# Two reorderings in a two-block transformer kernel: a step's row sums behind its side work, and a gain row behind the rests of the weights

## Chip, cores and metric
The kernel runs on one core of a Trainium2 chip. The metric is the device time of one execution in microseconds (us), the median of several runs. Engines are called by the profile's names: PE is TensorE (matrix products; PEld is its weight load), DVE is VectorE, ACT is ScalarE, POOL is GpSimd, and SP is the engine that issues most of the transfers.

## What is computed
Two blocks of two layers each run one after the other on 256 tokens (two tiles of 128, `NT = 2`) with a model width of 1024. The first block has a latent stream `x` and a context stream `ctx`; the second has one stream, with a mixture of experts at its end. What matters here:

```python
mod_l = silu(c) @ w_mod[l] + b_mod[l]            # first block: six rows of 1024 per layer
mod   = c_act @ w_ada[layer] + b_ada[layer]      # second block: a_shift, a_scale, a_gate, f_shift, ...
x_lat = x_lat + g1_l * rmsnorm(m_l, norm_mix_post[l])
f_l   = rmsnorm(x_lat, norm_ffn_pre[l]) * (1.0 + sc2_l) + sh2_l
x_lat = x_lat + g2_l * rmsnorm(swiglu(f_l, w_gate[l], w_up[l], w_down[l]), norm_ffn_post[l])
h     = h + f_gate * swiglu_2(u, ffn_w_gate[0], ffn_w_up[0], ffn_w_down[0])
```

`swiglu(h, wg, wu, wd)` is `(silu(h @ wg) * (h @ wu)) @ wd` with an inner width of 2816.

## The kernel before
**Exact products from three.** A float32 operand is split into an upper part, rounded by ACT (`high_*`), and a lower rest, which DVE subtracts (`low_*`). `products3` (lines 553 to 555) then adds three products: upper by upper, upper by rest, rest by upper. So each tile of weights costs a transfer (SP), an upper part (ACT, 1.9 us) and a rest (DVE, 2.3 us) before PE can use it.

**A dense line** (`class Line`) is one swiglu. It runs in steps of 256 inner columns, 11 steps per stream: the first line has two streams (22 steps), the second and third have one each (11 steps). The first lies at about 370 to 780 us, the second at 1036 to 1230, the third at 1375 to 1560. In step `n` PE does `up(n, 0)` and `up(n, 1)` (gate and up products of the two token tiles, 24 products each), small transposes `turn` of the hidden values through PSUM bank 6, and `downs(n - 1)` (24 products). DVE and ACT work on the next weights and the last hidden values. `fetch_w(n + 2)` (four transfers, 2 MB) and `fetch_d(n + 1)` (one, 1 MB) are issued by SP, each behind the semaphore that frees its buffer: the first behind `up(n, 1)`, the second behind `downs(n - 1)`. Each engine works through its instructions strictly in the order in which the program writes them, SP too.

**Side work.** `beside(n)` advances a generator by one piece, three times per step. In the first line it holds the norms, residual sums and transposes of the tokens of the other stream (`beside_first`): steps 0 to 5 and, after a pause, steps 12 to 17. In the second and third lines it is over after step 0.

**Row sums.** The modulation rows of the second block are row sums of `w_dots` times the condition, done by DVE in the lines. One `dot` multiplies a 128x1024 tile by the condition and adds up each row (112 in all; `tensor_tensor_reduce`, the rows `CUSTOM_DVE_ANT_0` of the profile), and then issues the next tile's transfer (512 KB) on SP into the buffer just read. There are two such buffers. `condition(n, long)` does two dots: with `long=False` ("early" below) after `split_h(n - 1, 1)`, only if no side work is under way, and with `long=True` ("late") after `split_h(n, 0)`, always. At n = 0 it only issues the first two transfers. A step without side work has four dots. The first line does 48, the second and third 32 each, up to their last step but two.

**The second output product** (`joint_out`, l = 1, at 1000 to 1050 us) multiplies the mixer's result by `w_out` in two halves of columns and two token tiles (`piece(j, t4)`). `row_gain` multiplies the gate row (broadcast from memory by POOL) by the norm row (transferred by SP) into a gain row, which `from_banks` uses in the token's residual sum. `split(1, h)` gives the two halves of the second half of `w_out`. `line.fetch_w(0)`, `high_w` and `low_w` prepare the first weights of the line that follows. `keep_busy` are products without use, which fill waits of PE.

Of the kernel before, what the change touches and what calls it, by code (L numbers as in the profile page):

```python
# [119 lines left out]
def build(nc, i, out):  # L120
# [150 lines left out]
    def bank_for_pe(b):  # L271
        pe.wait(*bank_free[b])
        return psum[:, b, :]
# [4 lines left out]
    def keep_busy(b, n):  # L278

        bk = bank_for_pe(b)  # L280
        for _ in range(n):
            t.matmul(bk[:, 0:256], ident[:], bc(ident[:], 1, 2), start=True, stop=True)
# [267 lines left out]
    def products3(out_, hi, lo, w_hi, w_lo, start, stop):  # L550

        hi, lo, w_hi, w_lo = (one_pass(z) for z in (hi, lo, w_hi, w_lo))
        t.matmul(out_, hi, w_hi, start=start, stop=False)  # L553
        t.matmul(out_, hi, w_lo, start=False, stop=False)  # L554
        return t.matmul(out_, lo, w_hi, start=False, stop=stop)  # L555
# [146 lines left out]
    def shape_condition():  # L702

        if broad[1]:
            broad[2] = ac.put(a.activation, cond, cond, ACT.Silu, after=[broad[1]])
            broad[1] = None

    def fetch_dot(limit):

        n = dot_asked[0]  # L710
        if n < limit:
            dot_asked[0] += 1
            slot = dot_slots[n % 2]
            sp.wait(slot.reader)
            nc.sync.dma_start(slot.ap[:], dot_rows[n // KD, :, n % KD, :]).then_inc(slot.sem, 16)
            slot.n += 16
            dot_there[n] = (slot.sem, slot.n)
# [126 lines left out]
    def finish_off(chain):  # L844
        for _ in chain:
            pass

    def to(chain, name):

        for r in chain:  # L850
            if r == name:
                return
        assert False, name

    def preload(function):

        loaded[0] += 1
        ac.put(a.activation, tables[:, loaded[0]:loaded[0] + 1], ident[:, 0:1], function)

    class Line:  # L860
# [128 lines left out]
        def run(self, streams, side, fetch_next, split_next, last_chain, waiting=None, root_first=False):  # L989

            self.streams, self.summed = streams, {}
            self.up_, self.down_, self.gate_, self.hidden_, self.turn_, self.h_split = {}, {}, {}, {}, {}, {}
            self.hi_free = pe.now()
            not_yet, beside_busy = [0], [bool(side)]

            def beside(n):
                if side and n >= not_yet[0]:  # L1000
                    r = next(side, "over")
                    not_yet[0] = r if isinstance(r, int) else 0
                    beside_busy[0] = r != "over" and not not_yet[0]

            def condition(n, long):

                if n == 0:
                    for slot in dot_slots:
                        slot.reader = self.up_[0, 1]
                        fetch_dot(self.dots)  # L1010
                elif n < end - 1 and (long or not beside_busy[0]):
                    for _ in range(2):
                        dot(self.dots)

            self.fetch_w(1)
            self.fetch_d(0)
            self.fetch_d(1)
            end = self.n - 1
            for n in range(self.n):
                self.up(n, 0)  # L1020
                if n == 0 and waiting:
                    finish_off(waiting)
                if n:
                    self.high_d(n - 1)
                    self.low_d(n - 1)
                if n == end:
                    self.high_d(n)
                self.high_w(n + 1, 0)
                self.gate(n, 0)
                if n:  # L1030
                    self.turn(n - 1, 1)
                if n == end:
                    self.low_d(n)
                self.low_w(n + 1, 0)
                self.hidden(n, 0)
                if n:
                    self.split_h(n - 1, 1)
                if n == end:
                    break
                if n == end - 1:  # L1040
                    self.downs(n - 1, (0, 1))
                    self.fetch_d(n + 1)
                if n:
                    condition(n, False)
                beside(n)
                self.up(n, 1)
                self.high_w(n + 1, 1)
                shape_condition()
                self.gate(n, 1)
                self.low_w(n + 1, 1)  # L1050
                self.hidden(n, 1)
                self.fetch_w(n + 2)
                self.turn(n, 0)
                self.split_h(n, 0)
                condition(n, True)
                beside(n)
                if n and n < end - 1:
                    self.downs(n - 1, (0, 1))
                    self.fetch_d(n + 1)
                if n == end - 1:  # L1060
                    fetch_next(0)
                beside(n)


            if side:
                finish_off(side)
            self.downs(end - 1, (0,), range(3))
            self.turn(end, 0)
            self.split_h(end, 0)
            self.downs(end - 1, (0,), range(3, 4))  # L1070
            self.downs(end, (0,))
            if split_next:
                split_next()
            p_ = end // self.per
            preload(ACT.Sqrt)
            chains = [last_chain(0, self.summed[p_, 0])]
            to(chains[0], "rooted" if root_first else "added")
            self.up(end, 1)
            fetch_next(1)
            preload(ACT.Silu)  # L1080
            self.gate(end, 1)
            if root_first:
                to(chains[0], "turn")
            self.hidden(end, 1)
            if not root_first:
                to(chains[0], "rooted")
            self.downs(end - 1, (1,), range(3))
            self.turn(end, 1)
            self.split_h(end, 1)
            self.downs(end - 1, (1,), range(3, 4))  # L1090
            to(chains[0], "late" if root_first else "turn")
            self.downs(end, (1,))
            fetch_next(2)
            return chains[0], last_chain(1, self.summed[p_, 1])
# [631 lines left out]
    def joint_out(l, cat4, keep, fetched, line, ready):  # L1726
# [33 lines left out]
        def split(j, half):  # L1760
            low_part(j, half, high_part(j, half))
# [13 lines left out]
        def piece(j, t4, between=None):  # L1775
            b = 2 * t4 + j - (4 if l == 1 else 0)
            bk, q = bank_for_pe(b), slice(t4 * P, (t4 + 1) * P)
            if (l, j, t4) == (1, 1, 2):
                keep_busy(b, 14)
            pe.wait(cat_split[t4])  # L1780
            for k in range(KD):
                if k == KD // 2 and between:
                    between()
                pe.wait(w_low[j, k // 4])
                mm = products3(bk, xhi[:, k, q], xlo[:, k, q], his[j][:, k, :], parts[j][k // 4][:, k % 4, :], k == 0, k == KD - 1)
            mm.then_inc(pe.sem, 1)
            pe.n += 1
            done[j, t4] = pe.now()

        def row_gain(u, n):  # L1790

            (_, s, blk), g_u = asked[u]
            g = grow[:, g_u, :]
            return g, [ve.put(v.tensor_tensor, g, g, prow[:, n, :], ALU.mult, after=[(s_row, rows[0]), (s_grow[g_u], grow_n[g_u])])]

        def own_banks(tt):
            return psum[:, 2 * tt:2 * tt + 2, :].rearrange("p b n -> p (b n)")
# [6 lines left out]
        def from_banks(s, tt, gain, sets, ready_, t0=0, early=(), busy=0):  # L1804

            t4 = 2 + tt if l else tt
            marks = (done[0, t4], done[1, t4])
            squared = list(early) + row_squares(tt, range(len(early), 2))
            return onward(s, tt, own_banks(tt), marks, squared, gain, spare[:, tt, :], sets,
                          (2 * tt, 2 * tt + 1), ready_, (2 * tt, 2 * tt + 1), t0, busy)  # L1810
# [21 lines left out]
        if l == 0:  # L1832
            gain = row_gain(0, 0)
# [37 lines left out]
            return squared, row_gain  # L1871
        keep.reader = pe.now()
        line.fetch_w(0)
        gain = row_gain(0, 0)
        split(1, 0)
        split(1, 1)
        sets = [[(1, xhi[:, :, tt * P:(tt + 1) * P], xlo[:, :, tt * P:(tt + 1) * P])] for tt in range(NT)]
# [3 lines left out]
        preload(ACT.Sqrt)  # L1881
        line.low_w(0, 0)
        piece(1, 2)
        c0 = from_banks(LAT, 0, gain, sets[0], ready[LAT])
        to(c0, "turn")
        line.low_w(0, 1)
# [793 lines left out]
    lat_squares, row_gain = joint_out(0, cat4, keep, fetched, line, there)  # L2680
# [63 lines left out]
    waiting, row_gain = joint_out(1, cat4, keep, fetched, line, there)  # L2744
# [618 lines left out]
    def moe(c):  # L3363
# [201 lines left out]
        with nc.Fori(0, NEXP) as e:  # L3565
            run(e)
# [75 lines left out]
```

## Time and profile before
| | us |
|---|---|
| median of 3 runs (lowest, highest) | 2771.52 (2766.29, 2773.17) |
| the profiled execution, its own time | 2772.69 |
| its span in the trace | 2771.4 |
| PE busy | 2620.0 (95%) |
| DVE busy | 2125.7 (77%) |
| ACT busy | 1486.9 (54%) |
| mean granted clock of PE | 0.969 |

A busy share is over the whole span. Much of it is the expert stage from 1770 us on, which the change doesn't touch. Of the chain that ended last, PE has 76%, DVE 13%, ACT 7%, DMA 2%. A row of a timeline gives start, duration, engine, line, operation, output and inputs, and in brackets how long the engine had been idle before it and what ended that. Lines 76, 553 to 555, 559 and 563 are helpers that issue most of the instructions, so rows are told apart by their tiles: `wslot` are gate and up weights, `dslot` down weights, `ld_hi` the down weights' upper part, `whi` the upper part of the others, `lhb` hidden values, `lhl` the lower rest of the transposed hidden values (the last operation of `split_h`), `dot` the tiles of the row sums.

### The profile page before, as it was taken

Reading aid. Unit: us, or ns where it says so; the run is one execution under the profiler, and the core shown is the slowest. Engines: PE = TensorE matmul, PEld = TensorE weight load, DVE = VectorE, ACT = ScalarE, POOL = GpSimd, SP = SyncE. Lnnn points to the kernel's source line nnn. Section 1 sums busy time; section 2 is a strip of 40 time slices with the busy share of each in tenths; the row PEclk is TensorE's granted clock in tenths of the full one; section 3 lists DMA queues with packets and bytes.
Section 4 is the critical chain, followed back from the end, with each engine's and each line's share of the span. In section 5 each row is a group of like instructions: output and inputs, shape, how many; then the busy total and the mean of one; then the engine's idle time right before and its main releaser. Section 6 shows DMA issues by size and latency. Waiting matters only on the chain.

```text
span 2771.4 us, 32200 instructions
## 1 busy us (share of the span) xinstructions
PE 2620.0 (95%) x12954; PEld 2132.0 (77%) x12954; DVE 2125.7 (77%) x2511; ACT 1486.9 (54%) x1665; POOL 110.6 (4%) x145
## 2 busy tenths in 40 slices
PE   7989998998998889999999999999999999999997
PEld 4767676887777678877788777788888888888886
DVE  4555566787647657868688667799999999999997
ACT  4332364445443244344633526677667776767674
POOL 4023100000000300000000000000000000000000
PEclk9999899999999989999999999999999999999999
DMA  7543545885553036952289340599999999999994
GB/s 277 183 156 122 190 166 191 299 304 203 180 210 122 1 121 240 327 197 95 96 305 328 136 175 31 185 371 364 351 367 368 353 362 365 362 354 367 369 364 189
DMA packets 290442, 675.24 MB, mean 244 GB/s; under 512 B 16726, under 2 KB 113158, under 8 KB 271344
## 3 DMA queue, kind: packets, MB, share of 16 engines
q1 hardware_dynamic: 285152, 664.35, 65.9%
q0 software_dynamic: 4272, 7.72, 1.1%
q8 instruction: 104, 1.70, 0.2%
q10 hardware_dynamic: 864, 1.06, 0.1%
q14 instruction: 50, 0.41, 0.0%
HBM read 671.98 MB, written 1.10 MB: 243 GB/s over the span
## 4 chain that ended last, share of the span: by engine, by line
PE 76%; DVE 13%; ACT 7%; DMA 2%; issue 1%; SPq 0%; POOL 0%; ACTq 0%; DVEq 0%; POOLq 0%
PE psum L553 21%; PE psum L555 21%; PE psum L554 21%; PE psum L76 7%; DVE wslot_r L563 3%; PE psum L1524 1%; PE psum L396 1%; ACT whi_r L76 1%; PE psum L1663 1%; DVE cacc L76 1%; PE psum L3063 1%; DVE dslot_r L563 1%; DMA first<-in_w_mod 1%; PE psum L2091 1%; DVE x L76 1%
## 5 line engine op out<-in xcount | busy, mean ns | idle before, releaser
L553 PE MATMUL psum<-whi_r,xhi_r 128*128 128x512 f32 (+1 forms) x752 | 295.5, 393 | 12.0 <-DVE wslot_r L563 5.4
L563 DVE TENSOR_TENSOR wslot_r<-wslot,whi_r 128x2048 fp32r<-128x2048 f32 (+1 forms) x114 | 255.6, 2252 | 61.5 <-ACT whi_r L76 61.1
L555 PE MATMUL psum<-whi_r,xlo_r 128*128 128x512 f32 (+1 forms) x752 | 290.4, 386 | 0.0
L554 PE MATMUL psum<-wslot_r,xhi_r 128*128 128x512 f32 (+1 forms) x736 | 283.7, 385 | 0.0
L76 ACT ACTIVATE whi_r<-wslot 128x2048 fp32r<-128x2048 f32 (+1 forms) x114 | 212.6, 1878 | 50.8 <-DMA wslot<-in_w_up 19.5
L563 DVE TENSOR_TENSOR wslot_r<-wslot,arena_r 128x2048 fp32r<-128x2048 f32 x85 | 194.0, 2288 | 18.7 <-ACT arena_r L3022 18.1
L563 DVE TENSOR_TENSOR ring_r<-ring,wide_r 128x2048 fp32r<-128x2048 f32 x84 | 191.8, 2288 | 17.8 <-ACT wide_r L3022 16.6
L563 DVE TENSOR_TENSOR wslot_r<-wslot,wide_r 128x2048 fp32r<-128x2048 f32 x83 | 189.7, 2288 | 16.7 <-ACT wide_r L3022 16.3
L563 DVE TENSOR_TENSOR ring_r<-ring,arena_r 128x2048 fp32r<-128x2048 f32 x84 | 191.6, 2287 | 11.6 <-ACT arena_r L3022 10.8
L3022 ACT ACTIVATE arena_r<-wslot 128x2048 fp32r<-128x2048 f32 x85 | 162.3, 1917 | 68.6 <-PE psum L555 45.6
L3022 ACT ACTIVATE arena_r<-ring 128x2048 fp32r<-128x2048 f32 x84 | 160.5, 1918 | 69.3 <-PE psum L555 48.5
L3022 ACT ACTIVATE wide_r<-ring 128x2048 fp32r<-128x2048 f32 x84 | 160.7, 1918 | 67.9 <-PE psum L555 45.5
L3022 ACT ACTIVATE wide_r<-wslot 128x2048 fp32r<-128x2048 f32 x83 | 158.7, 1918 | 71.3 <-PE psum L555 49.9
L553 PEld LDWEIGHTS psum<-whi_r,xhi_r 128*128 128x128 f32 x752 | 144.8, 193 | 47.7 <-DVE dslot_r L563 4.4
L555 PEld LDWEIGHTS psum<-whi_r,xlo_r 128*128 128x128 f32 x752 | 143.9, 191 | 27.8
L554 PEld LDWEIGHTS psum<-wslot_r,xhi_r 128*128 128x128 f32 x736 | 141.3, 192 | 25.6
L76 ACT ACTIVATE ld_hi_r<-dslot 128x2048 fp32r<-128x2048 f32 x44 | 83.8, 1912 | 139.5 <-PE psum L555 139.5
L563 DVE TENSOR_TENSOR dslot_r<-dslot,ld_hi_r 128x2048 fp32r<-128x2048 f32 x44 | 100.6, 2291 | 74.3 <-ACT ld_hi_r L76 74.3
L76 DVE CUSTOM_DVE_ANT_0 dot<-dot,stage 128x1024 f32<-128x1024 f32 x112 | 134.1, 1220 | 19.1 <-DMA dot<-in_w_dots 18.9
L553 PE MATMUL psum<-ld_hi_r,lhT_r 128*128 128x512 f32 x352 | 144.1, 409 | 1.4 <-DVE lhl_r L563 1.4
L555 PE MATMUL psum<-ld_hi_r,lhl_r 128*128 128x512 f32 x352 | 140.4, 399 | 0.0
L554 PE MATMUL psum<-dslot_r,lhT_r 128*128 128x512 f32 x352 | 140.1, 398 | 0.0
(540 smaller groups left out, 6334.5 us busy)
## 6 DMA issues: line engine op xcount, KB each, us to landing
wslot<-in_moe_w_gate SPq DMA_DIRECT2D x29, 2048.0 KB, 8.0
ring<-in_moe_w_down SPq DMA_DIRECT2D x29, 2048.0 KB, 8.3
dot<-in_w_dots SPq DMA_DIRECT2D x112, 512.0 KB, 6.1
wslot<-in_moe_w_up SPq DMA_DIRECT2D x28, 2048.0 KB, 8.5
ring<-in_moe_w_up SPq DMA_DIRECT2D x28, 2048.0 KB, 8.8
ring<-in_moe_w_gate SPq DMA_DIRECT2D x27, 2048.0 KB, 8.2
wslot<-in_moe_w_down SPq DMA_DIRECT2D x27, 2048.0 KB, 8.1
dslot<-in_w_mod SPq DMA_DIRECT2D x42, 1024.0 KB, 4.8
```

The costliest lines, as they stand in the source:

```text
L76: f(*a, **k).then_inc(self.sem, 1)
L396: mm = t.matmul(psum[32 * g:32 * g + 32, MB, :], cs[:, k, :], slot.ap[:, g * 512:(g + 1) * 512], start=fresh, stop=ends, tile_position=(0, ...
L553: t.matmul(out_, hi, w_hi, start=start, stop=False)
L554: t.matmul(out_, hi, w_lo, start=False, stop=False)
L555: return t.matmul(out_, lo, w_hi, start=False, stop=stop)
L563: return v.tensor_tensor(one_pass(lo), src, one_pass(hi), ALU.subtract)
L1524: mm = t.matmul(psum[:, 3, h * HD:(h + 1) * HD], PTj[:, buf, c0:c0 + P], kvd[:, kb, 128 + g * HD:128 + (g + 1) * HD], start=(kb == 0), sto ...
L1663: mm = t.matmul(o[:, h * HD:(h + 1) * HD], dec[:, d, h, :], xdt[:, d, h * HD:(h + 1) * HD], start=(d == 0), stop=(d == 1))
L2091: mm = t.matmul(psum[:, 6, (h % 8) * HD:(h % 8 + 1) * HD], PkT[:, buf, c0:c0 + P], vals(br, kb, h // 4), start=(kb == 0), stop=(kb == nb - 1))
L3022: a.activation(one_pass(hi_of(c, g, half)), raw(c, g, half), ACT.Copy).then_inc(a_high, 1)
L3063: mm = t.transpose(psum[:, 4, k * P:(k + 1) * P], hb4[:, k:512:4], ident[:])
```

## The change
In `Line.run` the late row sums keep their place at n = 0 (where they only issue transfers) and move for all other steps behind the last `beside(n)`, that is behind the step's side work and behind `downs(n - 1)` and `fetch_d(n + 1)`. In `joint_out` for l = 1 the product that makes the gain row moves from in front of `split(1, 0)` to behind `line.low_w(0, 0)` and `piece(1, 2)`. No operation is added or taken away.

```diff
                 self.turn(n, 0)
                 self.split_h(n, 0)
-                condition(n, True)
+                if n == 0:
+                    condition(n, True)
                 beside(n)
                 if n and n < end - 1:
                     self.downs(n - 1, (0, 1))
                     self.fetch_d(n + 1)
                 if n == end - 1:
                     fetch_next(0)
                 beside(n)
+                if n:
+                    condition(n, True)
...
         keep.reader = pe.now()
         line.fetch_w(0)
-        gain = row_gain(0, 0)
         split(1, 0)
         split(1, 1)
...
         line.low_w(0, 0)
         piece(1, 2)
+        gain = row_gain(0, 0)
         c0 = from_banks(LAT, 0, gain, sets[0], ready[LAT])
```

## Rows read from the trace of the kernel before

**Rows 1.** Busy time by stretch: PE, PEld, DVE, ACT, POOL; clock, DMA share, GB/s.
```profile
370.00:580.00 210.00, 194.46 (x848) 158.98 (x848) 153.35 (x215) 98.30 (x107) 1.08 (x2) 0.97 0.71 248
1050.00:1130.00 80.00, 80.00 (x362) 66.25 (x362) 64.82 (x80) 33.48 (x29) 0.00 (x0) 1.00 0.82 286
```

**Rows 2.** Chain of waits, 380 to 720 us: start, duration, what.
```profile
407.91 1.13 DVE dot L76
...
453.78 1.14 DVE dot L76
...
627.78 1.14 DVE dot L76
...
692.50 1.14 DVE dot L76
```

**Rows 3.** PE's timeline in the first line: rows with idle time before them.
```profile
423.29 0.71 PE L76 MATMUL psum<-c_ident,ysb 128*128 128x128 f32 x4 [2.11 <-DVE lhl_r L563]
...
465.22 0.70 PE L76 MATMUL psum<-c_ident,lhb 128*128 128x128 f32 x2 [4.89 <-DVE lhl_r L563]
...
482.67 1.12 PE L76 MATMUL psum<-c_ident,ysb 128*128 128x128 f32 x4 [3.86 <-DVE lhl_r L563]
...
644.20 0.51 PE L76 MATMUL psum<-c_ident,lhb 128*128 128x128 f32 x2 [2.02 <-DVE lhl_r L563]
...
669.06 0.71 PE L76 MATMUL psum<-c_ident,ysb 128*128 128x128 f32 x4 [1.50 <-DVE lhl_r L563]
...
706.75 0.71 PE L76 MATMUL psum<-c_ident,ysb 128*128 128x128 f32 x4 [2.82 <-DVE lhl_r L563]
```

**Rows 4.** Busy time by stretch behind two of these gaps; the clock is third last.
```profile
424.10:427.50 3.40, 3.40 (x10) 2.62 (x9) 2.71 (x8) 0.63 (x1) 0.00 (x0) 0.50 1.08 379
...
644.20:648.20 4.00, 4.00 (x18) 3.35 (x19) 0.73 (x4) 3.13 (x4) 0.00 (x0) 1.00 1.08 371
```

**Rows 5.** SP's timeline in the second line: transfers issued.
```profile
1089.02 3.25 SPq L715 DMA_DIRECT2D dot<-in_w_dots  x2
1092.31 0.43 SPq L898 DMA_DIRECT2D dslot<-in_w_down  x1
...
1174.13 0.43 SPq L898 DMA_DIRECT2D dslot<-in_w_down  x1
```

**Rows 6.** DMA issues at 1089.02, 1092.31 and 1174.13: KB, us to landing.
```profile
dot<-in_w_dots SPq DMA_DIRECT2D x1, 512.0 KB, 9.0
...
dslot<-in_w_down SPq DMA_DIRECT2D x1, 1024.0 KB, 9.3
...
dslot<-in_w_down SPq DMA_DIRECT2D x1, 1024.0 KB, 9.0
```

**Rows 7.** ACT's timeline in the second line.
```profile
1089.16 1.92 ACT L76 ACTIVATE ld_hi_r<-dslot 128x2048 fp32r<-128x2048 f32 x1 [5.39 <-PE psum L555]
1094.02 1.92 ACT L76 ACTIVATE whi_r<-wslot 128x2048 fp32r<-128x2048 f32 x1 [2.95 <-DMA wslot<-in_w_up]
...
1106.05 1.92 ACT L76 ACTIVATE ld_hi_r<-dslot 128x2048 fp32r<-128x2048 f32 x1 [5.39 <-PE psum L555]
```

**Rows 8.** DVE's timeline, first line and second line.
```profile
414.30 2.29 DVE L563 TENSOR_TENSOR dslot_r<-dslot,ld_hi_r 128x2048 fp32r<-128x2048 f32 x1 [3.22 <-ACT ld_hi_r L76]
...
1083.27 1.22 DVE L76 CUSTOM_DVE_ANT_0 dot<-dot,stage 128x1024 f32<-128x1024 f32 x1
...
1099.30 1.22 DVE L76 CUSTOM_DVE_ANT_0 dot<-dot,stage 128x1024 f32<-128x1024 f32 x1
...
1165.72 1.22 DVE L76 CUSTOM_DVE_ANT_0 dot<-dot,stage 128x1024 f32<-128x1024 f32 x1
```

**Rows 9.** Timelines of DVE, PE and ACT in the second output product.
```profile
1012.84 1.23 DVE L76 TENSOR_TENSOR grow<-grow,prow 128x1024 f32<-128x1024 f32 x1 [7.34 <-DMA prow<-in_norm_ffn_post]
...
1016.32 0.50 PE L553 MATMUL psum<-whi_r,xhi_r 128*128 128x512 f32 x1 [2.34 <-DVE dslot_r L563]
...
1018.24 1.92 ACT L76 ACTIVATE first_hi_r<-wslot 128x2048 fp32r<-128x2048 f32 x1 [0.81 <-DMA wslot<-in_w_up]
```

## Prediction
> **What bounds the kernel now.** I read the chain of waits first, then busy time by stretch, then the timelines of PE, DVE, ACT and SP inside the dense lines, and last the transfers. TensorE sets the end nearly everywhere: in the second dense line it is busy without a gap, 80.00 of 80 us, while DVE is busy for 64.82 [rows 1]. The third line repeats this. In the first line (370 to 790 us) it is not so: TensorE does 194.46 of 210 us in its first half, and the chain of waits leaves it for DVE and ACT, the moved row sums among them (at 407.91, 453.78, 627.78 and 692.50) [rows 1, 2]. The gaps are on TensorE's own timeline, each ended by `lhl_r`, the lower rest that frees bank 6 for the next transpose: 2.11, 4.89, 3.86, 2.02, 1.50 and 2.82 us [rows 3]. Behind that of 2.11 us the granted clock is at its lower level, 1.2 GHz (0.50), for 3.4 us; behind that of 2.02 us it stays at 1.00 [rows 4]. A product lasts twice as long at the lower level, so each such stretch costs 1.7 us more.
>
> **Part 1, row sums behind the side work, on DVE.** No instruction is added or removed: the row sums remain, at 1.22 us each [rows 8]. Per step n >= 1 two of them (2.3 us, with a closing sum of 0.5 us now and then) move from behind `split_h(n, 0)` to behind the step's last `beside`. Where no side work is left, DVE's order doesn't change at all. Where there is, the side's small DVE operations run 2.3 us sooner, so do ACT's scaling and `high_d` behind them, and the row sums fall into the time in which DVE waits for `ld_hi`. DVE shows this hole: the sums at 407.91 are on the chain [rows 2], end at 410.2, and then DVE waits 3.22 us for ACT's `ld_hi` until 414.30 [rows 8]. Step by step:
> - Step 1: DVE's chain comes 2.3 us sooner, but the next transposes also wait for `up(2, 1)` through gate, hidden and split (some 1.5 us, as the gap of 1.50 us shows [rows 3]): 2.11 us becomes 1.5, gain 0.6.
> - Step 3: the sums at 453.78 lead to the gap of 4.89 us. The whole 2.3 us are gained.
> - Step 4: DVE waits there for TensorE's transposes, not for the sums. The 3.86 us stay, gain 0.
> - Step 13: the sums at 627.78 and their closing operations are 2.8 us in front of the tile's norm. 2.0 us are gained at 644.20, and the other 0.8 at the gap after it, some 15 us later, which DVE's weights' rests end.
> - Step 15: the sums move into the wait for `ld_hi`. Gain 0.
> - Step 16: the sums up to 692.50 lead to the gap of 2.82 us, whose floor is again some 1.1 to 1.5. Gain 1.7.
> - Step 17: now the sums stand behind the gain row at the step's end and hold back `low_d`, where TensorE's reserve was 1.3 us. Loss 0.9.
> Sum: 0.6 + 2.3 + 2.8 + 1.7 - 0.9 = 6.5 us gained. Of the low stretches behind the gaps of 2.11 and 2.82 us one or both should go, since gaps of 1.50 and 2.02 us had none: 1.7 to 3.4 us at best; I take 1.7. **First line: 8.2 us faster**, between 3 (the floors are higher) and 11.
>
> **Part 1, the same move on SP.** `dot` also issues the next row's transfer, and SP works in order. Before, both transfers of a step were issued as soon as the sums were done, and `fetch_d(n + 1)` (1 MB of down weights) behind them: at 1089.02 the two rows, at 1092.31 the weights [rows 5]. Now `fetch_d` stands first. It waits for `downs(n - 1)`, which end when ACT's `ld_hi` starts, 1089.16 [rows 7], and the second sum was done only at 1091.9, so the weights go out about 3 us sooner and the rows behind them. The transfers are at that time queued up: the first row landed 9.0 us after its issue (1098.0), the weights 9.3 after theirs (1101.6) [rows 6]. With the second row, 1.2 us behind the first (an estimate: half a MB), the landings follow the order of issue: 1098.0, 1099.2, 1101.6. So 1 MB is worth 2.4 us, and with the weights first the rows land at 1100.4 and 1101.6.
> Who waits: the next step's two sums, at 1099.30 and 1.14 behind it [rows 8]. They had 1.3 and 1.2 us of reserve, and now wait for about 1.2. Behind them on DVE are `low_w(n + 1, 1)`, `hidden(n, 1)`, `split_h(n, 0)`; behind them on SP is `fetch_w(n + 2)`, which already lands just in time (ACT waits 2.95 us for it at 1094.02 [rows 7]). One such delay is hidden by reserve. The question is whether it adds up. A round of transfers, from the end of a step's early sums (the second starts at 1083.27, at 1165.72) to the landing of its weights, took 1084.4 to 1101.6 in the first and 1166.9 to 1183.1 in the last of six steps [rows 5, 6, 8]: 17.2 and 16.2, mean 16.6 us. Before, the sums didn't wait for the end of it. Now the last thing to land is the row that the second sum needs, so a round is closed: 16.6 + 1.2 (that sum) = 17.8 us, against TensorE's 16.9 per step (1089.16 to 1106.05 [rows 7]). TensorE's transposes of the second tile half came at about 1100.1 (5.9 before 1106.05) and needed the split that ended at 1099.3: reserve 0.8 us, which the first two waits use up. Then each step with four sums costs 0.9 us: seven such steps (n = 2 to 8), 6.2 us in the second line and the same in the third: **12.4 us slower**, from 0 (rounds shorter than 15.7 us) to 20 (17.2 each).
> In the first line steps 6 to 12 also have four sums, but `fetch_w` goes there at TensorE's pace and the reserve in front of the split is 3 us: I count 0 (at most 2). On POOL four of the late sums' steps store a finished gate row; POOL does nothing else of weight there, and the row is read only in the next stage: 0.
> The Trainium skill ("DMA: Bandwidth & Descriptors", Queues, rings and completion order) says that each DMA engine consumes descriptors in ring order, but that completion is not first-in first-out per issuing engine. By the first half the rows wait for all of the weights, as in the sum; by the second a row could overtake. The order of landings just given agrees with the first.
>
> **Part 2, the gain row.** `gain` waits 7.34 us for the norm rows, until 1012.84, and takes 1.23; the two rests of `w_out`, which need nothing of it, stand behind it, and TensorE's piece waits 2.34 us for them until 1016.32. Moved behind `low_w(0, 0)` and `piece(1, 2)`, the rests come 8 us sooner and the piece 2.3. But the chain that leads on from there starts at ACT, which waits for the line's first weights until 1018.24 [rows 9], takes 1.92 us for their upper part and then a table load of 1.3, so it squares from 1021.6 on, both halves by 1022.7; the piece ended at about 1022.0 (24 products of 0.23 us from 1016.32), so ACT was no earlier anyway. The gain row lies in the time in which DVE waits for those squares. What TensorE wins it stands idle some 10 us later, in front of the first tile's transposes, which wait for ACT and DVE. I count 0: at best 0.3, at worst 1.7, if that new gap brings the lower clock. SP's order doesn't change (the gain issues nothing).
>
> **Sum.** -8.2 + 12.4 + 0 = +4.2 us on the profiled execution's 2772.69 us (span 2771.4 and 1.3 around it): 2776.9, I say **2777**. That execution lies in the spread of the runs (median 2771.52, 2766.29 to 2773.17). About 0.3%, 8.3 us, is what a measurement can tell from no change.
>
> **Rivals.**
> - *Only the gain.* Landings don't bind: TensorE's pace keeps the rounds at 16.9 because a later start finds an emptier queue. For it: the six rounds vary by 1 us, and at 15.7 the drift is nil. Against it: the early sums had only 1.2 us of reserve and the weights take 2.4. Then -8.2: 2764.5. 22%.
> - *Slower by more than can be missed.* The closed round decides in lines two and three from the step on in which the split comes behind TensorE's transposes. At the 17.2 us of the first round it loses 1.5 us per step, 14 steps, 20 us less the 8.2: 2785; gaps of 2 us would bring lower clock on top. For it: the first round itself, and no reserve left in the early sums. 22%.
> - *Nothing moves.* The side work gets its 2.3 us but other gaps give them back (ACT's tables, the clock's phase), and DMA reserve suffices: 2772. 8%.
> - *The forecast case*, -2 to +10 us around +4.2: 48%, own range 2770 to 2782.
>
> **How the numbers follow.** Faster by over 0.3%: half of the first rival and a little of the forecast case, 0.13. Slower: the second rival and a sixth of the forecast case, 0.30. The rest, 0.57, within. For 8 in 10: 2763 to 2787.
>
> **What would show it.** In the changed trace: SP issues `dslot` before the two rows in each step; the row sums behind `split_h(n - 1, 1)` in the second line wait for DMA (before: none there), 1 us and more; ACT's `ld_hi` rows in that line come every 17.5 to 17.8 us instead of 16.9; TensorE has gaps of about 0.9 us there. In the first line the gaps at 465, 644 and 706 us shrink by 2.3, 2.0 and 1.7, that at 482 stays. TensorE's piece after the fill starts at about 1014, and the next stage no sooner than before. I am wrong if `ld_hi` keeps 16.9 us in line two, or if the first line doesn't get shorter by 5 us or more.

## The result and the profile after

| | before | changed |
|---|---|---|
| median, lowest and highest (us) | 2770.81 (2766.29, 2773.17) | 2788.36 (2782.30, 2791.43) |
| ratio, with its 95% interval | | 1.0048 (1.0030, 1.0066) |
| span in the trace | 2771.4 | 2790.1 |
| mean granted clock | 0.969 | 0.969 |

The medians are those of six runs of each kernel. The change makes the kernel slower, by 13.3 us by the ratio (8.3 to 18.3) and 17.5 by the medians. Forecast was 4.2 us slower: the side is right, the size is a third of the measured one by the ratio and a quarter by the medians. The changed median lies above the prediction's range of 2763 to 2787 us; by the ratio on the 2771.5 us of before it would be 2784.8, inside that range and outside the forecast case's own 2770 to 2782.

The chain that ended last is where one looks first. The part of the page after that gives its shares; before, DMA had 2% of it and the rows' transfers had no entry of their own.

```profile
PE 66%; DVE 14%; DMA 9%; ACT 6%; SPq 3%; issue 1%; POOL 0%; ACTq 0%; DVEq 0%; POOLq 0%
PE psum L553 18%; PE psum L555 17%; PE psum L554 17%; PE psum L76 7%; DMA dot<-in_w_dots 6%; DVE wslot_r L563 3%; DVE dot L76 2%; SPq L887 1%; PE psum L1527 1%; SPq L898 1%; PE psum L396 1%; DMA wslot<-in_w_up 1%; ACT whi_r L76 1%; PE psum L2094 1%; DVE cacc L76 1%
```

Busy time by stretch in the same stretches as [rows 1], and the clock behind two gaps that answer to those of [rows 4]: in the first line TensorE is busy for 2.8 us more of 210, the second has lost its full 80 us, and no low clock is left behind the gap at 417.74.

```profile
370.00:580.00 210.00, 197.25 (x865) 161.00 (x864) 153.42 (x210) 99.88 (x102) 1.07 (x2) 0.98 0.72 249
...
1050.00:1130.00 80.00, 78.43 (x351) 64.08 (x350) 61.02 (x77) 30.14 (x24) 0.00 (x0) 1.00 0.82 295
...
417.70:421.70 4.00, 3.96 (x19) 3.37 (x20) 2.06 (x5) 0.63 (x1) 0.00 (x0) 1.00 1.02 352
```

TensorE's timeline in the first line after, rows with idle time before them, to be laid beside [rows 3]. 2.11 has become 1.49, 4.89 has become 2.62, 3.86 stays, 2.82 has become 1.49, and 0.94 is new at step 17, all as forecast. But 2.02 has not gone (2.48), and 0.91 at 583.88 is new.

```profile
417.74 0.71 PE L76 MATMUL psum<-c_ident,ysb 128*128 128x128 f32 x4 [1.49 <-DVE lhl_r L563]
...
455.77 0.51 PE L76 MATMUL psum<-c_ident,lhb 128*128 128x128 f32 x2 [2.62 <-DVE lhl_r L563]
...
473.43 0.91 PE L76 MATMUL psum<-c_ident,ysb 128*128 128x128 f32 x4 [3.86 <-DVE lhl_r L563]
...
583.88 0.51 PE L76 MATMUL psum<-c_ident,lhb 128*128 128x128 f32 x2 [0.91 <-DVE lhl_r L563]
...
638.27 0.50 PE L76 MATMUL psum<-c_ident,lhb 128*128 128x128 f32 x2 [2.48 <-DVE lhl_r L563]
...
699.11 0.71 PE L76 MATMUL psum<-c_ident,ysb 128*128 128x128 f32 x4 [1.49 <-DVE lhl_r L563]
...
717.91 0.51 PE L76 MATMUL psum<-c_ident,lhb 128*128 128x128 f32 x2 [0.94 <-DVE lhl_r L563]
```

The second line after, first SP: `fetch_d` (L898) at 1099.92, the two rows behind it at 1102.42; in [rows 5] it was the other way round. The transfers issued there took, to their landing, 10.1 us and 8.9 us (median of two).

```profile
1099.92 2.46 SPq L898 DMA_DIRECT2D dslot<-in_w_down  x1
1102.42 1.34 SPq L715 DMA_DIRECT2D dot<-in_w_dots  x2
```
```profile
dslot<-in_w_down SPq DMA_DIRECT2D x1, 1024.0 KB, 10.1
...
dot<-in_w_dots SPq DMA_DIRECT2D x2, 512.0 KB, 8.9
```

DVE in the same round: the early sum at 1111.27 had to wait 1.05 us for its row, a wait that the same sum at 1099.30 in [rows 8] did not have. It comes in every step of the line from n = 2 to n = 8.

```profile
1109.80 0.42 DVE L563 TENSOR_TENSOR lhl_r<-psum,lhT_r 128x256 fp32r<-128x256 f32 x1
1111.27 1.22 DVE L76 CUSTOM_DVE_ANT_0 dot<-dot,stage 128x1024 f32<-128x1024 f32 x1 [1.05 <-DMA dot<-in_w_dots]
...
1112.51 1.23 DVE L76 CUSTOM_DVE_ANT_0 dot<-dot,stage 128x1024 f32<-128x1024 f32 x1
```

The transfers don't fill the round in either kernel. From 1112 to 1113 us, while the next rows and weights can't yet be issued, the DMA share is 0.01; before, it was 0.10 at the same place of the round (1100 to 1101 us). So the round is long because its parts wait for one another, not because the DMA engines are always full.

ACT behind it: `ld_hi` came every 16.9 us [rows 7] and now has 17.57 and 17.93 us between these three, and `whi` waits 4.13 and 4.48 us for weights that `fetch_w` asked for late.

```profile
1080.88 1.92 ACT L76 ACTIVATE ld_hi_r<-dslot 128x2048 fp32r<-128x2048 f32 x1 [5.39 <-PE psum L555]
1086.92 1.92 ACT L76 ACTIVATE whi_r<-wslot 128x2048 fp32r<-128x2048 f32 x1 [4.13 <-DMA wslot<-in_w_up]
...
1098.45 1.92 ACT L76 ACTIVATE ld_hi_r<-dslot 128x2048 fp32r<-128x2048 f32 x1 [6.08 <-PE psum L555]
1104.85 1.92 ACT L76 ACTIVATE whi_r<-wslot 128x2048 fp32r<-128x2048 f32 x1 [4.48 <-DMA wslot<-in_w_up]
...
1116.38 1.92 ACT L76 ACTIVATE ld_hi_r<-dslot 128x2048 fp32r<-128x2048 f32 x1 [6.44 <-PE psum L555]
```

TensorE's timeline in the second output product after: the wait of 2.34 us in front of the piece [rows 9] is gone, and in its place stands one of 2.04 us in front of the next transposes, which wait for ACT.

```profile
1021.62 1.30 PE L76 MATMUL psum<-c_ident,ysb 128*128 128x128 f32 x8 [2.04 <-ACT ysb L76]
```

**A yardstick for each line.** The first `ld_hi` of a line and the one of its last-but-one step (the 21st of the first line, the tenth of the second and third) mark the line's length. In the trace of before, in order of the lines: 371.1, 152.0 and 152.1 us.

```profile
394.59 1.90 ACT L76 ACTIVATE ld_hi_r<-dslot 128x2048 fp32r<-128x2048 f32 x1
765.72 1.91 ACT L76 ACTIVATE ld_hi_r<-dslot 128x2048 fp32r<-128x2048 f32 x1
...
1055.35 1.91 ACT L76 ACTIVATE ld_hi_r<-dslot 128x2048 fp32r<-128x2048 f32 x1
1207.36 1.91 ACT L76 ACTIVATE ld_hi_r<-dslot 128x2048 fp32r<-128x2048 f32 x1
1384.99 1.91 ACT L76 ACTIVATE ld_hi_r<-dslot 128x2048 fp32r<-128x2048 f32 x1
1537.04 1.91 ACT L76 ACTIVATE ld_hi_r<-dslot 128x2048 fp32r<-128x2048 f32 x1
```

After: 368.1, 160.9 and 161.6 us.

```profile
389.62 1.90 ACT L76 ACTIVATE ld_hi_r<-dslot 128x2048 fp32r<-128x2048 f32 x1
757.74 1.91 ACT L76 ACTIVATE ld_hi_r<-dslot 128x2048 fp32r<-128x2048 f32 x1
1047.04 1.91 ACT L76 ACTIVATE ld_hi_r<-dslot 128x2048 fp32r<-128x2048 f32 x1
1207.97 1.91 ACT L76 ACTIVATE ld_hi_r<-dslot 128x2048 fp32r<-128x2048 f32 x1
1390.13 1.91 ACT L76 ACTIVATE ld_hi_r<-dslot 128x2048 fp32r<-128x2048 f32 x1
1551.69 1.91 ACT L76 ACTIVATE ld_hi_r<-dslot 128x2048 fp32r<-128x2048 f32 x1
```

So the lines account for -3.0 + 8.9 + 9.5 = +15.4 us. The two profiled executions differ by 18.7. The other 3.3 us are a sum of larger parts: -5.0 in front of the first line, -0.3 between the first and the second (the gain row's place), +4.5 between the second and the third, and +4.1 behind the third. The change touches none of these but the second. e2 below shows parts of the same size: the kernel with the gain row alone was profiled at a span of 2778.0 us, 6.6 above before, and its median is that of before.

### The profile page after: what moved, and what is told of

It is laid out like the page before. It is cut to its first block, busy times and chain, and to the rows that moved or that the text cites. A ratio compares the mean times of both kernels' runs of the same rounds, so it can differ in the third digit from the quotient of the medians.

```text
span 2790.1 us, 32200 instructions
## 1 busy us (share of the span) xinstructions
PE 2627.2 (94%) x12954; PEld 2134.3 (76%) x12954; DVE 2129.2 (76%) x2511; ACT 1488.4 (53%) x1665; POOL 110.3 (4%) x145
## 4 chain that ended last, share of the span: by engine, by line
PE 66%; DVE 14%; DMA 9%; ACT 6%; SPq 3%; issue 1%; POOL 0%; ACTq 0%; DVEq 0%; POOLq 0%
PE psum L553 18%; PE psum L555 17%; PE psum L554 17%; PE psum L76 7%; DMA dot<-in_w_dots 6%; DVE wslot_r L563 3%; DVE dot L76 2%; SPq L887 1%; PE psum L1527 1%; SPq L898 1%; PE psum L396 1%; DMA wslot<-in_w_up 1%; ACT whi_r L76 1%; PE psum L2094 1%; DVE cacc L76 1%
## 5 line engine op out<-in xcount | busy, mean ns | idle before, releaser
L563 DVE TENSOR_TENSOR wslot_r<-wslot,arena_r 128x2048 fp32r<-128x2048 f32 x85 | 194.1, 2288 | 16.1 <-ACT arena_r L3025 15.1
L563 DVE TENSOR_TENSOR ring_r<-ring,wide_r 128x2048 fp32r<-128x2048 f32 x84 | 191.8, 2288 | 16.4 <-ACT wide_r L3025 15.2
L563 DVE TENSOR_TENSOR wslot_r<-wslot,wide_r 128x2048 fp32r<-128x2048 f32 x83 | 189.6, 2288 | 18.8 <-ACT wide_r L3025 17.8
L3025 ACT ACTIVATE wide_r<-ring 128x2048 fp32r<-128x2048 f32 x84 | 160.5, 1918 | 69.5 <-PE psum L555 51.2
L555 PE MATMUL psum<-arena_r,xf_lo_r 128*128 128x512 f32 x340 | 132.8, 391 | 0.0
```

The source lines that it names most:

```text
L563: return v.tensor_tensor(one_pass(lo), src, one_pass(hi), ALU.subtract)
L3025: a.activation(one_pass(hi_of(c, g, half)), raw(c, g, half), ACT.Copy).then_inc(a_high, 1)
```

## The experiments

Line lengths are by the yardstick above, in us. Each experiment's ratio is against the kernel before on the same chip.

| kernel | median | ratio (95%) | line 1 | line 2 | line 3 |
|---|---|---|---|---|---|
| before (trace) | 2771 to 2773 | | 371.1 | 152.0 | 152.1 |
| changed | 2788.36 | 1.0048 (1.0030, 1.0066) | 368.1 | 160.9 | 161.6 |
| e1: DVE new, SP old | 2765.04 | 0.9974 (0.9958, 0.9990) | 362.3 | 152.0 | 152.6 |
| e2: gain row alone | 2769.68 | 0.9999 (0.9984, 1.0014) | 371.2 | 152.0 | 152.0 |
| e4: DVE old, SP new | 2793.25 | 1.0078 (1.0061, 1.0095) | 374.2 | 160.5 | 162.0 |
| e5: first line only | 2770.69 | 0.9997 (0.9985, 1.0009) | 368.0 | 152.0 | 152.0 |
| e6: half rows | 2763.47 | 0.9960 (0.9945, 0.9975) | 364.6 | 152.0 | 152.0 |
| e7: steps 1 to 5 | 2781.05 | 1.0028 (1.0014, 1.0042) | 365.7 | 159.5 | 156.9 |
| e8: e1, old from step 17 | 2767.17 | 0.9975 (0.9961, 0.9989) | 361.0 | 152.2 | 152.0 |
| e9: rows on POOL | 2772.13 | 1.0000 (0.9983, 1.0016) | 364.4 | 155.6 | 155.2 |
| e10: steps 6 to 8 | 2769.06 | 0.9981 (0.9966, 0.9997) | 368.2 | 156.5 | 155.0 |
| e11: steps 1 to 7 | 2786.43 | 1.0050 (1.0030, 1.0071) | 365.9 | 159.2 | 164.3 |
| e12: e1 without gain row | 2762.41 | 0.9960 (0.9942, 0.9977) | 362.3 | 152.0 | 152.0 |

The theory: DVE's new order is a gain in the first line, SP's new order is a loss in all three, and the loss comes from bytes in the queue. The rival: DVE's order, or the clock, makes the loss. The forecast counted parts one by one ("term" below is one part of that sum); the experiments take them apart.

**DVE's order without SP's (e1).** In the changed kernel:

```diff
                 if n and n < end - 1:
                     self.downs(n - 1, (0, 1))
-                    self.fetch_d(n + 1)
...
                 if n:
                     condition(n, True)
+                if n and n < end - 1:
+                    self.fetch_d(n + 1)
```

> The changed kernel with fetch_d(n + 1) issued behind the late row sums, so that SP's order is again that of before (two rows, then 1 MB of down weights) while DVE's order is the changed one. Theory (the loss is SP's order: the rows stand behind the weights in the queue and the next step's early sums wait for them): ACT's ld_hi rows in the second and third line come every 16.9 us again, TensorE's gaps of 0.4 to 2.0 us there are gone, the two lines give back 8.9 and 9.6 us. The first line keeps the 3 us that it won. Total about 3 us below the kernel before (2766 to 2771), 15 to 20 below the changed one. Rival (the loss is DVE's order, or the phase of the clock, and the queue only shows it): the lines stay at 161 us from first to last ld_hi instead of 152, total 2782 to 2790.

Measured: 2765.04 us, 7.2 faster than before (2.8 to 11.6) and 20 to 23 faster than the changed kernel. The second and third line are back at 152. The rival falls. The total is just below the expected 2766 to 2771. The first line is 8.8 us shorter than before, not 3: the expectation took it from the changed kernel, and so missed that SP's order costs 5.8 us there too. In the first line of e1 the gap at step 13 is gone (2.0 us), and the one after it, 3.66 us at 659.54 before, is smaller by 0.4 of the 0.8 that was forecast. TensorE's timeline of e1, the whole of its gaps from 560 to 656 us:

```profile
648.09 0.69 PE L76 MATMUL psum<-c_ident,ysb 128*128 128x128 f32 x2 [3.26 <-DVE lhl_r L563]
```

**SP's order without DVE's (e4).** In the kernel before, the late sums stay, and their two transfers are issued at the end of the step, behind `fetch_d`.

```diff
-                        dot(self.dots)
+                        dot(self.dots, not long)
...
                 beside(n)
+                if n and n < end - 1:
+                    for _ in range(2):
+                        fetch_dot(self.dots)
```

> The kernel before with SP's order alone: the late sums stay where they were on DVE, the transfers of the next two rows are issued at the step's end, behind fetch_d. Theory: ld_hi every 17.5 us and more in the second and third line, about 9 us lost in each, nothing won in the first: 18 us slower than before, 2786 to 2793, at or above the changed kernel. Rival (DVE's order decides): ld_hi stays at 16.9 and the total within 3 us of before.

Measured: 2793.25 us, 21.6 slower (16.9 to 26.3): 8.5 and 10.0 us in the second and third line as expected, and 3.1 in the first, where the expectation had no loss. With e1 this closes the square. In the second and third line SP's order by itself makes the whole loss (8.5 and 10.0 against 8.9 and 9.5). In the first line the two orders don't simply add up: -8.8 (e1) and +3.1 (e4) make -5.7, and the changed kernel has -3.0. SP's order costs 3.1 us there behind DVE's old order and 5.8 behind the new one; in steps 6 to 11 e4 loses 0.2 us and the changed kernel 1.9.

**The gain row alone (e2).** Only the second hunk of the diff.

> The kernel before with part 2 alone (the gain row behind the weights' rests). Theory of the prediction: TensorE's piece starts 2.3 us sooner and the first tile's transposes no sooner, 0 us in total (0.3 better to 1.7 worse). Rival (the 4.5 us that the changed kernel lost between the second and third line, and 4.0 behind the third, at lower granted clock, belong to this part): the total is 3 us or more slower.

Measured: ratio 0.9999 (0.9984, 1.0014), so nothing within 4 us. Its profiled execution lost 5.5 us between the second and third line and 3.9 behind the third (by the yardstick), as the changed kernel's did, at a lower clock (0.70 from 1300 to 1345 us, before 0.81), and its median still doesn't move: those differences are one execution's and not the gain row's.

**First line only (e5).** `first` is true where a line has two streams.

```diff
-                if n == 0:
+                if n == 0 or not first:
                     condition(n, True)
...
-                if n:
+                if n and first:
                     condition(n, True)
```

> The changed kernel with the late sums at the step's end in the first line only, at the old place in the second and third; part 2 is in it. Theory: the second and third line as before (152 us from first to last ld_hi), the first line 3 us shorter as in the changed kernel: 2766 to 2770. Against the first kernel of this set it keeps the new order on SP in the first line, which the theory prices at 2 us (steps 6 to 12 of the changed kernel lost 1.9 us). Rival: the 4 to 5 us that the changed kernel lost outside the lines stay here too, and the total is 2774 or more.

Measured: 2770.69 us, no difference from before (-4.2 to +2.5), the second and third line at 152.0, the first at 368.0 as in the changed kernel. Against e1, which differs only in SP's order in the first line (in the other two no side work is left, so both run both engines' old order), that is 5.7 us by the lines and 5.7 by the medians. The price of SP's order in the first line is shown, and the 2 us of theory are wrong (the rival's 2774 or more is wrong too). ACT's timeline says where it is paid. The first fence is e1 at step 12, where the side work sets in again; the second is the changed kernel at the same step.

```profile
605.46 1.92 ACT L76 ACTIVATE ld_hi_r<-dslot 128x2048 fp32r<-128x2048 f32 x1 [2.97 <-PE psum L555]
607.28 1.90 ACT L76 ACTIVATE whi_r<-wslot 128x2048 fp32r<-128x2048 f32 x1
...
625.14 1.90 ACT L76 ACTIVATE ld_hi_r<-dslot 128x2048 fp32r<-128x2048 f32 x1
```
```profile
607.20 1.92 ACT L76 ACTIVATE ld_hi_r<-dslot 128x2048 fp32r<-128x2048 f32 x1 [2.48 <-PE psum L555]
613.19 1.92 ACT L76 ACTIVATE whi_r<-wslot 128x2048 fp32r<-128x2048 f32 x1 [4.07 <-DMA wslot<-in_w_up]
...
630.67 1.90 ACT L76 ACTIVATE ld_hi_r<-dslot 128x2048 fp32r<-128x2048 f32 x1
```

In e1 `whi` follows `ld_hi` at once; in the changed kernel it waits 4.07 us for weights, and the norms of the side work, which stand behind it on ACT and DVE, are late: 23.5 us from `ld_hi` to `ld_hi` against 19.7. The rounds of steps 6 to 11 had built up that delay (`whi` comes 2.5, 3.2, 5.3, 5.8, 6.6 and 5.7 us behind `ld_hi`, in e1 always 1.8 but for 2.2 at the first) while TensorE lost only 1.9 us of it (in e1 nothing).

**Half the bytes (e6).** In the changed kernel a row's transfer brings 512 of 1024 columns, and the sum is made twice over them; the modulation rows are then not those of the reference.

```diff
-            nc.sync.dma_start(slot.ap[:], dot_rows[n // KD, :, n % KD, :])...
+            nc.sync.dma_start(slot.ap[:, 0:512], dot_rows[n // KD, :, n % KD, 0:512])...
```

> The changed kernel with half of each row's bytes: a row transfer brings 256 KB instead of 512, and its sum is made in two operations over the same half, so that DVE's time stays about the same (the modulation rows are then not those of the reference). Theory (a closed round of transfers: 5 MB per step, 17.6 us from the end of a step's early sums over rows, weights and rows to the next): four half rows take 4 x 0.6 = 2.4 us out of the round, 15.2 us is below TensorE's 16.9, ld_hi comes every 16.9 us in all three lines. The second and third line last 152 us, the first 362 as with SP's old order (in the changed kernel 368), and the total is that of the first kernel of the first set, 2760 to 2768. Rival (the loss is the wait for the semaphore and the order of SP's instructions, not bytes): ld_hi stays at 17.6 us and the total at 2780 or more.

Measured: 2763.47 us, 11.1 faster than before (6.9 to 15.2), all rounds of the second and third line at 16.9, and step 12 of the first at 19.7 as in e1. SP's order is the changed one, and it costs nothing here. So it is the length of the round, not the order as such: a smaller row shortens it, whether by its bytes alone or by what a shorter transfer also saves the transfers behind it. The first line is 364.6 instead of 362: a gap of 4.15 instead of 3.85 us at step 4 and one step at 28.9 instead of 27.2 are left unexplained.

**The rows on their own queue (e9).** `fetch_dot` in the changed kernel:

```diff
-            sp.wait(slot.reader)
-            nc.sync.dma_start(slot.ap[:], ...
+            po.wait(slot.reader)
+            nc.gpsimd.dma_start(slot.ap[:], ...
```

> The changed kernel with the rows' transfers issued by POOL on its own queue instead of SP; the weights stay on SP. Theory: the rows no longer stand behind the weights' 1 MB, and SP's fetch_w no longer waits for the early sums, so the round is open: ld_hi every 16.9 us, 152 us in the second and third line, the first as with SP's old order, total 2760 to 2768. Rival (one set of DMA engines serves both queues at about the rate at which it is now filled, so a row queued second still comes second or the rows slow the weights): 17.3 us and more per step, 2780 and more.

Measured: 2772.13 us, as before (-4.7 to +4.4). The middle of the expectation holds: from the second `ld_hi` to the ninth the period is 16.9 us again. The edit does two things at once, and the run doesn't separate them: the rows leave the queue of the 1 MB, and SP issues `fetch_w` without waiting for the sums. That a row gets past the weights shows at one place, by little: weights issued at 1114.76 land at 1124.1, a row issued by POOL at 1115.16 lands at 1123.5. Its edges don't: the first period is 18.8 us in the second line and 19.1 in the third, the last 18.4 and 17.8. At the start POOL issues two rows while SP's queue still holds the first weights, and ACT's `whi` at 1052.66 waits 5.46 us for its own (in the changed kernel 3.23 at that place). The first line is 2.1 us longer than e1's. The total is therefore above the 2768 that was expected.

**A part of the steps (e7, e10, e11).** All three are the changed kernel with the late sums at the step's end only in the steps named, in the second and third line.

```diff
-                if n == 0:
+                behind = n and (len(streams) == 2 or n < 6)    # e7; e10: n > 5; e11: n < 8
+                if not behind:
                     condition(n, True)
```

> The changed kernel, but in the second and third line the late sums stand at the step's end in steps 1 to 5 only and at the old place from step 6 on (the first line is unchanged from the changed kernel). Theory: three rounds of 17.6 us in each line lose 0.7 each, 2 to 2.5 us per line; with SP's old order from step 6 the queue catches up, ld_hi comes every 16.9 us again, and the loss of the last two steps (1.3 and 3.6 us in the changed kernel's second line), which is the lag meeting the step in which the down products come before up(n, 1), is gone. Each line 154.5 us from first to last ld_hi, total 4 to 5 us above the version with the first line only, 2773 to 2777. Rival (the end of the line costs 4 to 5 us by itself, whatever came before, or the lag stays): 157 us and more per line, 2780.

Measured: 2781.05 us, missed by 4. The lines are 159.5 and 156.9, both longer than the expected 154.5; lines and total are what the rival said (157 and more, 2780). Five periods are long (17.8 18.0 18.2 17.8 18.0 in the second line), not three, since a round's delay arrives two steps after it; then come 16.9 and, in the last, 19.0. SP's old order stops the loss but doesn't give the queue its reserve back. That made me form the theory of the next two.

> The changed kernel, but in the second and third line the late sums stand at the step's end in steps 6 to 8 only (the other half of the version with steps 1 to 5). Theory now (the lag of the rounds, once there, isn't given back, because the old round of 16.6 us is hardly shorter than TensorE's 16.9, and it is paid a second time, with 1.5 to 4 us, where the last-but-one step has no up(n, 1) in front of the down products): the first two rounds are free as in the other versions, one is lost at 0.7 to 1.0, and the last two steps cost 1 to 3 us: 154 to 156 us per line against 152 of before, total 2771 to 2777. Rival (the end costs its 4.9 us by itself wherever the new order reaches it): 157 us per line, 2778 and more. Rival two (the lag needs many steps to build up): 152 to 153 us, 2767 to 2770.

Measured: 2769.06 us, and lines of 156.5 and 155.0. Every period is 16.9 us but the last, 21.3 and 19.8. So TensorE need not lose anything before the end for the end to cost 3 to 4.4 us, which is near what the first rival said; my theory had one late round and 1 to 3 us at the end. But the lag is there, and grows, before it is paid: `whi` comes 3.3, 4.1 and 5.4 us behind `ld_hi` in the last three steps. And the rival's "wherever the new order reaches it" is too narrow: in e7 the old order stands from step 6 on, and the end still costs 2.1 and 1.5 us. The second rival (the lag needs many steps) is refuted by the lines, though the total falls into its range. The total came out lower than the lines make it (5.3 us below before, 0.8 to 9.4, against about 5 above in the profiled execution); that stays open. The shares of busy time don't show this cost, ACT's and TensorE's timelines do. The fences are of e10.

```profile
1185.39 1.92 ACT L76 ACTIVATE ld_hi_r<-dslot 128x2048 fp32r<-128x2048 f32 x1 [5.39 <-PE psum L555]
1190.83 1.92 ACT L76 ACTIVATE whi_r<-wslot 128x2048 fp32r<-128x2048 f32 x1 [3.53 <-DMA wslot<-in_w_up]
```
```profile
1196.25 0.50 PE L553 MATMUL psum<-ld_hi_r,lhT_r 128*128 128x512 f32 x1 [2.52 <-DVE lhl_r L563]
```
```profile
1196.20:1200.00 3.80, 3.75 (x11) 2.98 (x12) 2.20 (x1) 0.00 (x0) 0.00 (x0) 0.68 0.00 0
```

At step 9, the last but one, `downs(8)` stand in front of `up(9, 1)` and not behind it, so TensorE needs the split of step 8 one product group (5.6 us) sooner. `whi` comes 5.4 us behind `ld_hi`, where before it followed 1.8 behind, and the split behind it is 2.5 us late. In ordinary steps `up(n, 1)` hides just this. Behind the gap the granted clock is a mix of its two levels (0.68), and takes another 1.2 of 3.8 us.

> The changed kernel with the late sums of step 8 alone (the last that has any in the second and third line) back at the old place. Theory: the periods before the last two stay at 17.6 us, and the last one, 20.5 us in the second line and 19.2 in the third of the changed kernel, keeps a part of its excess, as in the version with steps 1 to 5 (19.0 and 18.4): 1 to 2 us less per line than the changed kernel, total 2783 to 2787. Rival (the last period's excess is wholly that of step 8's own order): 16.9 in the last period, 3 to 4 us less per line, 2780 and less. Rival two (all of it is lag): nothing less, 2786 to 2790.

Measured: 2786.43 us; the last periods are 20.3 and 22.5 us. Step 8's own order is not what costs; the second rival ("all of it is lag") fits, if lag includes what ordinary steps hide. It is the periods that say so: the total lies in the range of the theory as well as in that of this rival. The third line at 164.3 is even longer than the changed kernel's.

**A better kernel (e8, e12).** Both start from e1: e8 sets the late sums back to the old place from step 17 on, e12 leaves the gain row where it was.

```diff
-                if n == 0:
+                behind = 0 < n < 17
+                if not behind:
                     condition(n, True)
```

> The kernel with DVE's new order and SP's old one, with the late sums back at the old place from step 17 on (only step 17 of the first line differs). Theory: the gap of 0.94 us at 712 us goes, nothing else changes: 1 us faster than that kernel, 2762 to 2766. Rival: the side work of step 17 comes 2.3 us later instead and a gap of 1 us or more opens behind it: same or slower.

> The kernel with DVE's new order and SP's old one, without part 2 (the gain row stands where it stood). Theory: part 2 is worth nothing here either: within 2 us of that kernel, 2763 to 2767. Rival (TensorE's earlier piece is worth its 2.3 us when the first line ends sooner, or its new gap costs a low clock): 2 to 5 us on one side.

Measured: e8 2767.17 us, e12 2762.41. In e8's trace the gap of 0.94 us is gone and the line is 1.3 us shorter; the time doesn't show it (0.9975 against 0.9974), and it is outside the expected 2762 to 2766. e12 is the fastest kernel that still makes the full rows, 11.1 us below before (6.4 to 16.1), but its interval overlaps e1's, the lines are alike, and e2 had priced the gain row at nothing. I take the three as equal: about 0.3% faster than before.

## Why the forecast was right in its side and short in its size

- **By the prediction's own tests.** It named two signs of being wrong. The first, `ld_hi` staying at 16.9 us in the second line, did not come. The second did: the first line got 3.0 us shorter and not 5 or more. The two terms below that were mis-sized both err to the same side, so the forecast's side is owed to the mechanism of the second and third line and not to errors that cancel.
- **First line, DVE's order: right.** Forecast -8.2 us, measured -8.8 (e1). The single steps came nearly as worked out: 2.11 to 1.50, 4.89 to 2.63, 3.86 unchanged, 2.02 gone, 3.66 to 3.26 (by 0.4 instead of 0.8), 2.82 to 1.49 (by 1.3 instead of 1.7), and 0.94 lost at step 17. That is 5.7 us of gaps where 6.5 were forecast. The clock made up for it: both low stretches went, behind the gaps of 2.11 and of 2.82 us (granted clock 0.58 over the 4 us behind the latter, now 1.00), where one of 1.7 us was counted. That the total is so near is partly luck.
- **First line, SP's order: wrong, and the first term that was mis-sized.** "I count 0 (at most 2)": it is +5.8 us (e1 against the changed kernel). I had set the reserve in front of the split, 3 us, against one delay. But the same closed round runs in steps 6 to 11, uses the reserve up, and hands its delay to step 12, where the side work has none: 3.8 of the 5.8 us fall in that period. The gain forecast for step 13 was there, and was paid out again by this.
- **Second and third line, the mechanism: right.** The round was forecast at 17.8 us, the second line's periods came at 17.6 mostly; the first early sum waits for about 1.05 us, where "about 1.2" was said. `ld_hi` at 17.5 to 17.8 was said, and gaps of 0.9 us (in the second line's ordinary steps they are 0.4 to 1.1). The prediction's order of landings, weights and then two rows, holds: by issue and time to landing the weights land at 1110.0, and the sum that needs the first row starts at 1111.27.
- **Second and third line, the size: too small, the second mis-sized term.** Forecast 6.2 us for each, measured 8.9 and 9.5. In the second line the first six late periods (17.6 17.9 17.6 17.6 17.6 18.2 against 16.9) cost 5.1 us together, near the forecast. The seventh, the last-but-one step's, costs 3.6 alone and was in no term. I had treated all steps alike, though the listing shows `downs(n - 1)` in another place for `n == end - 1`. e10 shows that this is paid even without any late period before. The third line loses in another proportion: four late ordinary periods (17.7 17.5 17.5 18.3) cost 3.4 us, and the last two (20.6 and 19.2) 6.0. In the first of these two the early sum at 1508.36 waits 2.58 us for its row, TensorE then has a gap of 1.81 us at 1524.80, and behind it the granted clock is 0.50 (1526 to 1528 us). Why that row is so late is open; e10 and e11 have such an early sum in the third line too (2.38 and 2.66).
- **Part 2: right.** What TensorE won in front of the piece it stood idle in front of the next transposes, as forecast. e2 says 0.9999.
- **The sum.** -8.8 + 5.8 + 8.9 + 9.5 + 0 = +15.4 us, inside the measured 8.3 to 18.3. Forecast: -8.2 + 0 + 6.2 + 6.2 = +4.2.
- **The rivals.** "Slower by more than can be missed" had the right place and point, the closed round in each step; its price of 1.5 us per step was wrong (0.7), and its 2785 came near the measured time only because what made up for it lay in the edges and in SP's order in the first line. "Only the gain" is what e1 does, at 2765.04 against the 2764.5 worked out for it.
- **The rule on queues.** The Trainium skill ("DMA: Bandwidth & Descriptors", Queues, rings and completion order) says that an engine consumes its descriptors in ring order. The trace agrees in the round shown above: on SP's queue the rows, issued behind the weights, land behind them (1111.3 against 1110.0), and in e9 the row from POOL's queue landed 0.6 us before weights that were issued 0.4 us sooner on SP's.

## What to carry to other kernels

When an instruction that also issues a transfer is moved, list the queue's new order by itself and price it by itself; here it cost 24 us and the move was meant for an order worth 9. Issue order and compute order can be moved apart, as in e1: then the move pays. And price a delay per step not only in the ordinary step but in each step whose order differs (the first, the last but one, the one where side work sets in): what the ordinary step hides is asked for there.

## What the runs showed of the hardware

- A second queue is not free: with rows on POOL's queue the steady rounds fit into 16.9 us, but ACT waited 5.46 us for a line's first weights, and the first period grew by 1.9 and 2.1 us (e9).
- Behind a gap of 2.52 us the granted clock was 0.68 over 3.8 us (e10), behind one of 1.49 it stayed at 1.00. The length of the one gap doesn't decide it: in the changed kernel the clock stayed at 1.00 behind a gap of 2.48 us (638.27) and fell to 0.50 behind one of 1.81 (1524.80).
- One profiled span can stand 6.6 us (0.24%) off while the median stays (e2), with a lower mean clock (0.965 against 0.969); that the clock's dips make all of it is not shown. The 22 executions of the kernel before that were measured beside e10 to e12 spread over 20 us (2763.98 to 2784.09). A difference of a few us in one pair of traces outside the changed code is no effect of it.
